# Every sixth gathered row of the first table: product on GpSimd, sum on ScalarE, the rest on VectorE

## What is computed

```python
scores = jnp.einsum('bshpd,hpnd->bshpn', q, sub_keys)
sv, si = lax.top_k(scores, PEER_TOPK)
...
gw = jax.nn.softmax(tv, axis=-1)
...
a = jnp.einsum('td,ted->te', xc, expert_u[ic])
a = jax.nn.gelu(a, approximate=False) * wc
return jnp.einsum('te,ted->td', a, expert_v[ic])
```

## Time and profile before

| | |
|---|---|
| median of 3 runs | 3429.58 us |
| the profiled execution | 3429.93 us |
| its span | 3428.2 us |
| VectorE busy | 2002.2 us (58%) |
| ScalarE busy | 481.8 us (14%) |
| GpSimd busy | 868.8 us (25%) |
| the 256 dots (L1708), busy | 322.8 + 249.9 us |
| the 256 gathers of the first table (L375), busy on GpSimd | 248.4 + 223.6 us |
| mean rate of all DMA | 271 GB/s |

### The profile page before, as it was taken

One profiled execution on the slowest core, in us unless ns is written; L12 is line 12 of the kernel. 1 busy time (PEld: TensorE's weight loads), 2 busy tenths in 40 slices (PEclk: granted clock), 3 DMA queues, 4 the chain that ended last, 5 costly groups with the idle time before them and its releaser, 6 DMA issues.

```text
span 3428.2 us, 29254 instructions
## 1 busy us (share of the span) xinstructions
PE 2633.6 (77%) x10654; PEld 1995.4 (58%) x10654; DVE 2002.2 (58%) x2593; ACT 481.8 (14%) x1020; POOL 868.8 (25%) x709
## 2 busy tenths in 40 slices
PE   8999988999999989998999999100013206999993
PEld 2488866888888868866888888100013105444441
DVE  4231956441554346813533126899999999655556
ACT  0100113010011020011100021000059603000000
POOL 1100000000000000000100003666667665544444
PEclk9999999999999999988999999555555555999996
DMA  9674435865875623222966339988898896999997
GB/s 370 219 278 147 147 135 216 341 247 202 346 312 207 275 85 135 99 72 90 422 264 267 137 145 365 355 360 355 366 383 360 359 382 196 349 401 380 386 395 278
DMA packets 155043, 927.97 MB, mean 271 GB/s; under 512 B 17344, under 2 KB 17344, under 8 KB 67520
## 3 DMA queue, kind: packets, MB, share of 16 engines
q0 software_dynamic: 101520, 605.07, 44.7%
q1 hardware_dynamic: 52992, 319.50, 24.6%
q10 hardware_dynamic: 432, 2.10, 0.2%
HBM read 922.41 MB, written 4.19 MB: 270 GB/s over the span
## 4 chain that ended last, share of the span: by engine, by line
PE 53%; DVE 29%; DMA 14%; issue 2%; POOL 1%; ACT 1%; DVEq 0%; POOLq 0%; ACTq 0%
PE G L393 43%; DMA acc<-v_rows,proj 11%; DVE aring L1708 8%; DVE ring L1708 7%; PE M L549 3%; DVE vec L1726 3%; DMA aring<-peer_u,proj 2%; DVE proj L1268 1%; PE G L487 1%; DVE proj L1739 1%; PE B L526 1%; POOL acc L381 1%; DMA aring<-ada 1%; PE M L501 1%; PE B L437 1%
## 5 line engine op out<-in xcount | busy, mean ns | idle before, releaser
L393 PE MATMUL G<-h,ring 128*128 128x256 f32 x5376 | 1189.5, 384 | 16.4 <-ACT h L858 14.8
L393 PEld LDWEIGHTS G<-h,ring 128*128 128x128 f32 x5376 | 1034.5, 193 | 163.1 <-issue 18.7
L342 POOL DMA_DIRECT2D aring<-ada x192 | 102.7, 535 | 1717.7 <-DVE acc L1174 840.8
L393 PE MATMUL G<-proj,ring 128*128 128x256 f32 x2080 | 465.3, 387 | 4.5 <-DVE proj L1508 1.6
L1726 DVE SCALAR_TENSOR_TENSOR vec<-acc,dots,vec 128x1024 f32<-128x1024 f32 x254 | 328.0, 1291 | 206.2 <-DMA acc<-v_rows,proj 203.3
L815 PE MATMUL M<-sq,mix 128*128 128x512 f32 x1024 | 442.0, 594 | 2.4 <-DMA sq<-v_blocks 1.3
L393 PEld LDWEIGHTS G<-proj,ring 128*128 128x128 f32 x2080 | 405.1, 195 | 63.8 <-issue 5.8
L1177 DVE SCALAR_TENSOR_TENSOR acc<-aring,cond,acc 128x2048 f32<-128x2048 f32 x135 | 317.5, 2351 | 146.1 <-DMA aring<-ada 139.8
L381 POOL DMA_INDIRECT acc<-v_rows,proj x256 | 293.3, 1146 | 301.7 <-DVE vec L1726 273.7
L815 PEld LDWEIGHTS M<-sq,mix 128*128 128x128 f32 x1024 | 195.2, 191 | 248.7 <-issue 245.1
L1708 DVE CUSTOM_DVE_ANT_0 aring<-sq,aring 128x2048 f32<-128x2048 f32 x144 | 322.8, 2288 | 28.4 <-DMA aring<-peer_u,proj 28.1
(11 more groups left out here) (292 smaller groups left out, 2032.9 us busy)
## 6 DMA issues: line engine op xcount, KB each, us to landing
ring<-weights SPq DMA_DIRECT2D x229, 1024.0 KB, 4.8
aring<-ada POOLq DMA_DIRECT2D x192, 1024.0 KB, 11.3
sq<-v_blocks SPq DMA_DIRECT2D x128, 512.0 KB, 6.6
acc<-v_rows,proj POOLq DMA_INDIRECT x256
aring<-peer_u,proj POOLq DMA_INDIRECT x144, 11.0
x<-xT SPq DMA_DIRECT2D x1, 2048.0 KB, 10.9
proj<-ctxT SPq DMA_DIRECT2D x1, 2048.0 KB, 17.9
x_kept<-acc SPq DMA_DIRECT2D x1, 2048.0 KB, 16.0
```

The source lines that it names most:

```text
L342: pool.dma_start(aring[:, slot, :], ada[a]).then_inc(ada_in[slot], 16)
L393: mm = nc.tensor.matmul(bank[:, 0:TOK], lhsT=ring[:, slot, weights_at + t * P:weights_at + (t + 1) * P], rhs=rhs[:, t, :], start=(t == 0), ...
```

## The change

Rows from 32 on with n mod 6 = 4 (34, 40, ..., 250: 37 of the 224) are no longer VectorE's. GpSimd multiplies the slot by `sq` in place, one 128x2048 `tensor_tensor`, right behind its gather of row n + 5 (`BEHIND`); ScalarE then sums the slot with a Copy activation that has an accumulator output into the same column of `dots`. Two new semaphores, `row_scaled` and `row_summed`, say how many rows have been multiplied and summed; whoever waited for all dots now waits for the two counts, and a gather into a slot whose last row was one of these waits for its sum. ScalarE's order is interleaved: sums of the first 96 rows stand ahead of `gate_exp(0)`; behind each `one_hots(g)` come the sums of rows 144 + 4g to 147 + 4g; `gate_exp(1)` moves from behind the last group to g = 20, ahead of the sums of rows 224 on.

```diff
+BEHIND = 5
+        def summed_on_act(n):
+            return n >= EARLY and n % 6 == 4
+        def act_rows(n):
+            return sum(summed_on_act(m) for m in range(n))
+        def dve_rows(n):
+            return n - act_rows(n)
...
-            sp.wait_ge(dot_done, 2 * NSLOT)
+            sp.wait_ge(dot_done, dve_rows(2 * NSLOT))
+            sp.wait_ge(row_scaled, act_rows(2 * NSLOT))
...
+            def scale_row(n):
+                pool.wait_ge(ht_copied, 4)
+                pool.wait_ge(u_in[row_slot(n)], 16 * row_count(n))
+                tk = n // NSLOT
+                nc.gpsimd.tensor_tensor(u_slot(n), u_slot(n), sq[:, tk * D:(tk + 1) * D], ALU.mult).then_inc(row_scaled, 1)
...
-                if 4 <= n < EARLY:
-                    pool.wait_ge(dot_done, n - 3)
-                elif n >= EARLY + 4:
-                    pool.wait_ge(dot_done, n - 7)
+                if 4 <= n < EARLY or n >= EARLY + 4:
+                    last = n - 4 if n < EARLY else n - 8
+                    if summed_on_act(last):
+                        pool.wait_ge(row_summed, act_rows(last + 1))
+                    else:
+                        pool.wait_ge(dot_done, dve_rows(last + 1))
                 where = bass.IndirectOffsetOnAxis(picks[:, n:n + 1], 0)
                 pool.indirect_dma_start(u_slot(n), None, peer_u, where).then_inc(u_in[row_slot(n)], 16)
+                if n >= BEHIND and summed_on_act(n - BEHIND):
+                    scale_row(n - BEHIND)
+            for n in range(2 * NSLOT - BEHIND, 2 * NSLOT):
+                if summed_on_act(n):
+                    scale_row(n)
...
             def dots_gelu(tk):
-                act.wait_ge(dot_done, NSLOT * (tk + 1))
+                act.wait_ge(dot_done, dve_rows(NSLOT * (tk + 1)))
+                act.wait_ge(row_summed, act_rows(NSLOT * (tk + 1)))
...
+            def sum_rows(first, last):
+                for n in range(first, last):
+                    if summed_on_act(n):
+                        act.wait_ge(row_scaled, act_rows(n + 1))
+                        tk = n // NSLOT
+                        nc.scalar.activation(u_slot(n), u_slot(n), ACT.Copy,
+                                             accum_out=dots[:, 0, tk, n % NSLOT:n % NSLOT + 1]).then_inc(row_summed, 1)
+            sum_rows(0, 6 * SEL)
             gate_exp(0)
             keep_picks(0)
+            sum_rows(6 * SEL, NSLOT)
             dots_gelu(0)
+            sum_rows(NSLOT, NSLOT + SEL)
             keep_coefs(0)
             act.wait_ge(turned_kept, 2)
+            row = lambda g: min(NSLOT + SEL + 4 * g, 2 * NSLOT)
             for g in range(P // 4):
                 one_hots(g)
                 if g > 0:
                     keep_mix(0, g - 1)
+                if row(g) == NSLOT + 6 * SEL:
+                    gate_exp(1)
+                sum_rows(row(g), row(g + 1))
             keep_mix(0, P // 4 - 1)
-            gate_exp(1)
             keep_picks(1)
             dots_gelu(1)
...
                 for n in range(b * SEL, (b + 1) * SEL):
-                    dot(n)
+                    if not summed_on_act(n):
+                        dot(n)
```

More of the change, by code:

```diff
@@ L278, in build @@
                                                             sem("coef_ready"), sem("v_added"))
+        row_scaled, row_summed = sem("row_scaled"), sem("row_summed")
         turned, turned_kept = sem("turned"), sem("turned_kept")
```

## The result

The changed kernel takes 3537.37 us (median of 4 runs, 3531.19 to 3540.01) against 3429.15 us: 1.0313 times as long, 95% interval 1.0295 to 1.033. The forecast was 3539 us, range 3450 to 3600. The profiled execution took 3540.01 us, its span is 3538.3 us, 110.1 us more than the span before.

A forecast was written before the change was run, and what follows sets the result against it. VectorE was taken to bound the stage of rows 32 to 255, with DMA next. Holds +71, lagging gathers +15 and the late gelu +23 gave +109 us on 3429.9 us: 3539 us, range 3450 to 3600.

The forecast's parts named there:

- Part 1 and 2: 37 dots off VectorE, 82 us; GpSimd products of 4.4 us replace 32 dots by holds, +71 us; five beside picks, zero.
- part 3: Gathers queued behind products on GpSimd make VectorE starve, 1.2 us per block: +15 us, ends 0 and 66.
- 98%: Sign after the change: VectorE's busy share stays at 98% though it has 37 dots fewer.
- Part 4: Sums on ScalarE, 37 x 2 = 74 us beside an engine mostly idle in this stage: nothing, except by order.
- Part 5: One-hot groups moved behind the rows' sums make the last gelu late: +23 us, ends 18 and 30.
- A: Rival: GpSimd reads without stopping VectorE; -73 us by the DMA bound, +23 us for the late gelu: 3380 us; 12%.
- B: Rival: no hold of VectorE, but a GpSimd product of 4.4 us: 3453 us; 12%.
- C: Rival: the hold is longer, 6.9 us, with starving at its upper end of 66 us: 3669 us; 8%.
- no more than 73 us are to be won: DMA limit in rows 32 to 255: 554 us at 424 GB/s against 627, capping the gain from relieving VectorE.

The follow-up runs named there:

- experiment 4: Changed kernel, but GpSimd copies the slot onto itself (one SBUF input) in place of the product: 3442.1 us.
- experiments 1: Changed kernel, but dots of rows 32 to 255 read the tokens' vectors from PSUM, where ScalarE copies them: 3411.1 us.
- experiment 3: Changed kernel, but three fills of the slot with 1.0, which read nothing, replace GpSimd's product: 3457.5 us.
- experiment 6: Changed kernel with the product behind gather n + 2, then n + 7, in place of n + 5: 3588.3 and 3567.6 us.
- experiment 5: Changed kernel, but only three rows' sums, not four, may stand behind each one-hot group: 3512.0 us.
- experiment 7: Changed kernel with dots from PSUM and three rows' sums per one-hot group: 3381.35 us; then also GpSimd rows n mod 16 = 3, 8, 13: 3386.23 us.

## Why the prediction was right

**Part 1 and 2.** Dots removed, -82, were certain. For the holds I had 32 x 2.2 = +71 net. Measured: +101 beside dots, +40 in picks, -82 removed, net +59. The product takes 4.50 us at least, against the 4.4 us estimated. Its length was met closer than its working deserved: 4.4 was two passes of 2.21, but one input in and out takes GpSimd 1.9 us in experiment 4, and no run splits the 4.5. That VectorE is held for nearly all of it was the bet, and experiments 1, 3 and 4 show it for the dots: no hold without the shared input, none without reading, and a hold that follows the length of the reading instruction. The Trainium skill states the exclusion (SBUF — State Buffer, Who interferes with whom); the trace now agrees on VectorE's side too, with dots of 6.58 us. Its price of 4497 ns for such an add (GPSIMD Engine Reference, Elementwise — side-by-side cycle accounting) agrees with the 4500 to 4530 ns of the products that nothing held.

The split was off, and two errors partly offset. Only five products were to run beside picks, at a net of zero; 13 did, because GpSimd's lag carries products behind a block's last dot. Besides the five they are rows with m mod 16 = 14, four, which part 3 had named, and 0, another four, which it had not. That took some 18 us off the sum. But in the picks a product costs 3.1 us, above the 2.2 of the removed dot, which put 11 us on. I had let only the two-input L1662 wait in the picks. A one-input CAST is held as well (up to 5.08 us), which the step did not have.

**Part 3.** The lag was put at +15, ends 0 and 66; VectorE's waits for landings are 22 us. They also bring VectorE's busy share to 95% from 2200 to 2900 us, where 98% was named as a sign. That the lag is a term of its own, and how it grows, experiment 6 shows.

**Part 4.** Nothing but order: in the changed kernel no gather's longest wait is for a sum. It held.

**Part 5.** +23 forecast, 25.6 us of waiting found; experiment 5 takes it away and with it 17 to 22 us of time. The groups took the 32.2 us of the working; VectorE had 8.8 us of dots left after the product of row 250, not 11.1.

**The sum.** +109 was forecast, +110 came in the profiled execution. So close a total is luck: the net of the holds was 12 us too high, the landings 7, the gelu 2 and the part behind it 2 us too low. The four terms and the order of their sizes are right.

**Rivals.** A falls with the 6.58 us dots. B did not happen. Experiment 3 comes near its case; it gives +36 us against the kernel before on its chip where B had +23, with 5.4 us of fills for B's product of 4.4 and with holds in the picks that B did not have, so B's working is neither shown nor refuted. C, a hold of 6.9 us, falls with 4.5. In rival A's price and the first paragraph, though, "no more than 73 us are to be won" rested on 424 GB/s of the fullest slices. In experiment 7, with the dots' holds gone and 15 us of waits for landings left, the stage still took 580 us, 47 us won: the mean rate from 2200 to 2760 us was 393 GB/s. So a mean over a stage has to be taken lower than its best slices; some 17 us of the 580 went to products that held picks.

## What to carry to other kernels

Before work goes to GpSimd, look at how its existing instructions run beside VectorE: a gather that takes 1.91 us beside one kind of instruction and 0.93 beside another had here already shown the exclusion, and the long reading instruction showed it the other way round. If the work must go there, move one input of VectorE's instruction to PSUM first; here that took off some 120 us, and together with ScalarE's order repaired it turned +113 us into a gain of 44. And when engines' orders are interleaved by hand, count what is left on the borrowed engine behind the last borrowed item: 25 us here.

## What the runs showed of the hardware that I had not expected

A CAST of 128x32 with one SBUF input waits for a GpSimd product (2.51 us for 0.18), while MAX8 and FIND_INDEX8 beside the same product do not (0.43 and 0.42 us as ever). The Trainium skill says that casts, copies and tensor_scalars can run in modes that take the port pair shared with GpSimd (SBUF — State Buffer, Who interferes with whom); this row agrees, and so do the fills of experiment 3: fills of 128x2048 (1.81 us) never held a dot, but a TENSOR_SCALAR of 0.175 us took up to 1.83 us beside them. And a dot whose record begins 0.28 us before the product's can still be the one that waits:

```profile
2334.54 6.95 DVE L1754 CUSTOM_DVE_ANT_0 aring<-sq,aring 128x2048 f32<-128x2048 f32 x1 [0.54 <-DMA aring<-peer_u,proj]
2334.82 4.50 POOL L386 TENSOR_TENSOR aring<-aring,sq 128x2048 f32<-128x2048 f32 x1
```

6.95 us are the product's 4.50, the dot's 2.29 and 0.16: who comes first is not to be read from the starts of two records so close together. A dot from PSUM takes the same 2.29 us as one from SBUF.
